# Attention beside a long convolution: one PSUM layout and one order of the turn against another

## What is computed

```
# attention: 4 heads, 2 maps each, 64 dims; latent queries see 256 + 1024 keys, context queries 256
s = einsum('bqhmd,bkhmd->bhmqk', q, k) * DIFF_SCALE
p = softmax(s, -1)
o = einsum('bhqk,bkhe->bqhe', p[:, :, 0] - lam * p[:, :, 1], v)      # then rms norm, * silu(gate)
# hyena: two long convolutions by FFT, 512 channels
z = x1 * fft_long_conv(v, kf[:, 0], bias[0]);  out = x2 * fft_long_conv(z, kf[:, 1], bias[1])
```

## Time and profile before

| | |
|---|---|
| median of 3 runs | 3829.0 us (3826.55 to 3842.98) |
| the profiled execution | 3828.31 us |
| its span, first to last instruction | 3826.5 us |
| mean granted TensorE clock | 0.953 of full speed |
| busy share of the span | TensorE 88%, VectorE 62%, ScalarE 28%, GpSimd 28% |

### The profile page before, as it was taken

One profiled execution on the slowest core, in us unless ns is written; L12 is line 12 of the kernel. 1 busy time (PEld: TensorE's weight loads), 2 busy tenths in 40 slices (PEclk: granted clock), 3 DMA queues, 4 the chain that ended last, 5 costly groups with the idle time before them and its releaser, 6 DMA issues. The chain is left out here.

```text
span 3826.5 us, 48036 instructions
## 1 busy us (share of the span) xinstructions
PE 3363.5 (88%) x18212; PEld 2736.8 (72%) x18212; DVE 2391.5 (62%) x3952; ACT 1088.9 (28%) x1980; POOL 1065.3 (28%) x766
## 2 busy tenths in 40 slices
PE   6999999999968885886997888999999588858698
PEld 2788888888758784654783576888888588845477
DVE  4134566765459986885554324557865489968765
ACT  2112222212245554332211211222221355523321
POOL 4233334333202322210122423433443022232121
PEclk8999999999979998998998899999999799989899
DMA  5354223223173222334426155323332633133441
GB/s 205 72 157 149 81 93 96 89 90 91 54 211 100 79 69 99 114 106 137 155 77 220 50 121 170 98 76 94 100 100 74 202 92 94 44 109 112 130 151 64
DMA packets 414889, 423.30 MB, mean 111 GB/s; under 512 B 57040, under 2 KB 351440, under 8 KB 413506
## 3 DMA queue, kind: packets, MB, share of 16 engines
q1 hardware_dynamic: 368676, 315.22, 28.5%
q10 hardware_dynamic: 45984, 105.01, 7.8%
HBM read 287.76 MB, written 124.01 MB: 108 GB/s over the span
## 5 line engine op out<-in xcount | busy, mean ns | idle before, releaser
L763 PE MATMUL l_p_acc<-l_u_hi,l_w_hi 128*128 128x512 f32 (+1 forms) x2208 | 605.8, 376 | 25.6 <-ACT l_p_stg L827 10.8
L763 PE MATMUL l_p_acc<-l_u_hi,l_w_lo 128*128 128x512 f32 (+1 forms) x2208 | 587.3, 367 | 0.0
L763 PE MATMUL l_p_acc<-l_u_lo,l_w_hi 128*128 128x512 f32 (+1 forms) x2208 | 586.4, 367 | 0.0
L763 PEld LDWEIGHTS l_p_acc<-l_u_hi,l_w_hi 128*128 128x128 f32 x2208 | 383.6, 189 | 102.5 <-issue 28.7
L676 POOL TENSOR_TENSOR l_w_hi<-l_wt,l_p_zero 128x1024 fp32r<-128x1024 f32 x100 | 199.6, 1996 | 916.4 <-PE l_p_acc L763 762.0
L763 PEld LDWEIGHTS l_p_acc<-l_u_hi,l_w_lo 128*128 128x128 f32 x2208 | 380.9, 189 | 71.7
L763 PEld LDWEIGHTS l_p_acc<-l_u_lo,l_w_hi 128*128 128x128 f32 x2208 | 380.5, 188 | 71.7
L1493 PE MATMUL l_at_pS<-l_at_k_hi,l_at_q 128*128 128x512 f32 (+1 forms) x400 | 165.8, 415 | 125.3 <-ACT l_at_prob L1609 69.9
L678 POOL TENSOR_TENSOR l_w_lo<-l_wt,l_w_hi 128x1024 fp32r<-128x1024 f32 x100 | 267.7, 2677 | 7.8
L1727 DVE TENSOR_REDUCE l_at_nmax<-l_at_pS 128x1 f32<-128x1280 f32 (+1 forms) x144 | 197.4, 1371 | 115.9 <-PE l_at_pS L1494 113.7
L2444 PE MATMUL l_o_pA<-l_o_w_hi,l_o_o_hi 128*128 128x512 f32 x576 | 223.6, 407 | 43.1 <-DVE l_o_o_lo L2554 31.2
(11 more groups left out here) (321 smaller groups left out, 6932.2 us busy)
## 6 DMA issues: line engine op xcount, KB each, us to landing
l_wt<-w_in SPq DMA_DIRECT2D x104, 512.0 KB, 3.9
l_n_wa<-w_ada SPq DMA_DIRECT2D x10, 2048.0 KB, 16.6
kf_d<-l_p_R SPq DMA_DIRECT2D x72, 256.0 KB, 3.7
xbc_d<-l_p_fin ACTq DMA_DIRECT2D x28, 640.0 KB, 3.0
l_at_K<-kf_d SPq DMA_DIRECT2D x64, 256.0 KB, 2.9
l_o_rows<-w_out SPq DMA_DIRECT2D x32, 512.0 KB, 4.5
l_o_oT<-o_d SPq DMA_DIRECT2D x16, 1024.0 KB, 6.8
qk_d<-l_p_late ACTq DMA_DIRECT2D x12, 1280.0 KB, 4.6
```

What stands on the lines that cost most here:

```text
L763: mm = pe.matmul(acc[:, a:a + w], (w_hi, w_lo)[wp][m % 2][:, k], (u_hi, u_lo)[up][:, k, t0 + c:t0 + c + w], start=(k == n == 0), stop=(k = ...
```

## The change

pS grows to six banks, three for each map (`MAP`), and both maps take their pieces in the same order, the 256-key piece last, with no wait on the exp of the other map. pO loses its own bank and moves into the unused half of the sixth bank, beside the last piece of map 1. So two waits are new: scores(i, 1) waits, ahead of its third piece, until norm(i-3) has read pO, and values(n) waits until exp(n+2, 1) has read that bank.

TensorE's turn becomes: values(i-3) (it was values(i-2), late in the turn); turn(i-2, 0); forward(n); turn(i-2, 1); scores(i, 1); the last batch of turn(i-2); turn_rows; scores(i+1, 0) (it was scores(i, 0), ahead of forward); backward(n). ScalarE's turn becomes: copy_back(n-1), exp(i, 0), norm(i-3), copy(i-2, 0), copy(i-2, 1), the last copy, exp(i, 1). VectorE's order stays.

```diff
@@ -1385,10 +1385,11 @@
-        pS = ps(nc, ctx, tag + "pS", 5 * BANK)
+        pS = ps(nc, ctx, tag + "pS", 6 * BANK)
+        pO = pS[:, 5 * BANK + CTX:5 * BANK + CTX + P]
         pT = ps(nc, ctx, tag + "pT", BANK)
-        pO = ps(nc, ctx, tag + "pO", BANK)
         pH = ps(nc, ctx, tag + "pH", BANK)
+        MAP = 3 * BANK
@@ -1485,11 +1486,10 @@ scores(n, m)
-                    pieces = [(0, CTX)] if q < CT else [(0, BANK), (BANK, BANK), (2 * BANK, CTX)] if m == 0 else [(CTX, BANK), (CTX + BANK, BANK), (0, CTX)]
-                    for c, w in pieces:
-                        out = pS[:, m * T + c:m * T + c + w]
-                        if w == CTX and q >= CT and n + m:
-                            pe.wait_ge(exped, 2 * n + m)
+                    for c, w in [(0, CTX)] if q < CT else [(0, BANK), (BANK, BANK), (2 * BANK, CTX)]:
+                        out = pS[:, m * MAP + c:m * MAP + c + w]
+                        if m == 1 and c == 2 * BANK and n >= 3:
+                            pe.wait_ge(scaled, n - 2)
@@ -1519,10 +1519,10 @@ values(n)
                     if n:
                         pe.wait_ge(scaled, n)
+                    pe.wait_ge(exped, 2 * min(n + 3, NU))
+                    pe.wait_ge(turned_copied, before[n + 1])
                     for kt in range(keys(q) // P):
-                        if kt % 4 == 0:
-                            pe.wait_ge(turned_copied, before[n] + kt // 4 + 1)
-                        mm = pe.matmul(pO[:, 0:P], mixT[:, kt], v_s[:, h % 2, kt], start=(kt == 0), stop=(kt == keys(q) // P - 1))
+                        mm = pe.matmul(pO, mixT[:, kt], v_s[:, h % 2, kt], start=(kt == 0), stop=(kt == keys(q) // P - 1))
@@ -1569,10 +1569,12 @@ TensorE's turns
                     turning = batches[i - 2] if 2 <= i < NU + 2 else 0
+                    if i == 0:
+                        scores(0, 0)
+                    if 3 <= i < NU + 3:
+                        values(i - 3)
                     if turning > 1:
                         turn(i - 2, 0, False)
-                    if i < NU:
-                        scores(i, 0)
                     if n is not None:
                         forward(n)
@@ -1581,7 +1583,6 @@
                     if turning:
                         turn(i - 2, turning - 1, i >= 4)
-                        values(i - 2)
@@ -1592,6 +1593,8 @@
                         turn_rows(r)
+                    if i + 1 < NU:
+                        scores(i + 1, 0)
                     if n is not None:
                         backward(n)
@@ -1644,14 +1647,14 @@ ScalarE's turns
                         copy_back(step_of(i - 1))
+                    if i < NU:
+                        exp(i, 0)
+                    if 3 <= i < NU + 3:
+                        norm(i - 3)
                     if turning > 1:
                         copy(i - 2, 0)
-                    if 3 <= i < NU + 3:
-                        norm(i - 3)
                     if turning > 2:
                         copy(i - 2, 1)
-                    if i < NU:
-                        exp(i, 0)
                     if turning:
                         copy(i - 2, turning - 1)
```

More of the change, by code:

```diff
@@ L1608, in exp @@
                         act.wait_ge(mixed, n + m - 1)
-                    act.activation(prob[:, (2 * n + m) % 3, 0:keys(q)], pS[:, m * T:m * T + keys(q)], ACT.Exp,
+                    act.activation(prob[:, (2 * n + m) % 3, 0:keys(q)], pS[:, m * MAP:m * MAP + keys(q)], ACT.Exp,
                                    bias=nmax[:, n % 2, m:m + 1], accum_out=sums[:, n % 4, m:m + 1]).then_inc(exped, 1)
@@ L1620, in norm @@
                     act.activation(small_sq[:, n % 2:n % 2 + 1], sums[:, n % 4, 0:1], ACT.Square, scale=math.sqrt(RMS_EPS)).then_inc(squared, 1)
-                    act.activation(junk[:], pO[:, 0:P], ACT.Square, accum_out=ss[:, n % 2:n % 2 + 1]).then_inc(squared, 1)
+                    act.activation(junk[:], pO, ACT.Square, accum_out=ss[:, n % 2:n % 2 + 1]).then_inc(squared, 1)
                     act.wait_ge(squared, 2 * n + 2)
@@ L1628, in norm @@
                         act.wait_ge(o_turned, n - 1)
-                    act.activation(o_t[:, n % 2], pO[:, 0:P], ACT.Copy, scale=rms[:, n % 2, 1:2]).then_inc(scaled, 1)
+                    act.activation(o_t[:, n % 2], pO, ACT.Copy, scale=rms[:, n % 2, 1:2]).then_inc(scaled, 1)
                 def copy_rows(n):
@@ L1726, in maximum @@
                     dve.wait_ge(scored, 2 * n + m + 1)
-                    dve.tensor_reduce(nmax[:, n % 2, m:m + 1], pS[:, m * T:m * T + keys(q)], AX.X, ALU.max, negate=True).then_inc(maxed, 1)
+                    dve.tensor_reduce(nmax[:, n % 2, m:m + 1], pS[:, m * MAP:m * MAP + keys(q)], AX.X, ALU.max, negate=True).then_inc(maxed, 1)
                 def combine(n):
```

## The result

The changed kernel took 3924.8 us (median of 4 runs, 3918.1 to 3928.2), against 3830.1 for the kernel before beside it: a ratio of 1.0231, 95% interval 1.0211 to 1.0250. It is slower, as forecast, but by 95 us where 50 were forecast, and so above the range's end of 3905. The profiled run took 3924.19 us, its span 3922.4, at a mean granted clock of 0.945 (0.953 before).

A forecast was written before the change was run, and what follows sets the result against it. It took VectorE and TensorE, both close to full in the attention and hyena stage, as the bound. Layer 1 +26.5, layer 0 +27.7 and first turns -3.2 made +51 on 3828.3: 3879, put down as 3878, range 3852 to 3905 us.

The forecast's parts named there:

- the chain: Inside a turn, from max(i,0) to max(i,1) through reduce, exp(i,0), norm(i-3), copy(i-2,0), transposes and a map: 6.69 us.
- D to M: Start of max(i,0) to that of max(i,1); before, 4.57, 4.73, 4.58, 6.71 us for s=(i-3) mod 4 of 3, 0, 1, 2.
- The floor: VectorE's time after the start of max(i,1), taken as before: 4.47, 6.13, 4.89, 4.78 us for s=3, 0, 1, 2.
- After the change TensorE is busy over 75% of each turn, more than in that stretch, so I keep 1.00: TensorE in the changed stage: granted clock stays 1.00, though an earlier stretch with a 2.91 us stall got 0.79.
- for s=2 nothing: Turns with (i-3) mod 4 = 2: VectorE waits nothing for max(i,1), turn stays 11.49 us.
- only s=3 grows there, by 0.35: Turns 3 to 13, row transposes waiting for the gate: only turns with s=3 grow further, by 0.35 us.
- 0 (bounds -6 to +6): Layer 0, twelve turns touching a unit of context (256 keys): no net change, bounds -6 to +6 us.
- short maps shorten the rest: Layer 0's turns touching a context unit: short maps offset a path ending at norm, about 4.9 against 4.57 to 4.73 us.
- Cost nothing: values(i-3) at the head of TensorE's turn, waiting for exp(i-1,1): no cost, with 0.3 us of cover.
- A: Rival, faster: VectorE runs at its floor and max(i,1) never waits, 3808 us; chance 0.04.
- B: Rival, no change: the chain exists without norm in it, D to M 5.28 us, time 3828 to 3832; chance 0.06.
- Case C: Rival, slower yet: TensorE's clock falls at its wait before turn(i-2,1), about 3985 us, or 3930 for half the turns; chance 0.05.

The follow-up runs named there:

- experiment 5: The changed kernel with forward's sixteen matmuls issued twice in every turn from 14 on: 3937.7 us, ratio 1.0274 to the kernel before.
- experiment 1: The changed kernel with ScalarE's old order (copy of batch 0, norm, copy of batch 1, exp of the first map): 3850.0 us, ratio 1.0041.
- experiment 10: The changed kernel with ScalarE's old order, turn_rows behind backward, and GpSimd's last level of an element waiting for VectorE's join: 3823.6 us, ratio 0.9969.

## Why the prediction was right in direction and wrong in size

The mechanism forecast, the chain, came as forecast. Its sum left out two things that came on top, the fall of the clock and the longer join, and priced several turns of layer 0 too low.

**Right.** The chain through exp(i,0), norm(i-3) and copy(i-2,0): 6.74 us measured against 6.69 summed. That nothing waits ahead of max(i+1,0) in late turns, that TensorE's idle moves to the transposes of mix, and that the values cost nothing in the late turns. They did wait, 0.62 us after turns 17, 21 and 25, where the prediction had a cover of 0.3 us, but with no effect on D to M. "The floor" after M was 0.15 too short in s=3 and s=1 (4.62 and 5.04 us).

**Wrong, in layer 1.** The forecast for the stage was 24.9 us (26.5 less 1.6 for the first turns); it grew by 45.1. By the same turns:

- Turns 16 to 30: 188.5 us measured, 175.4 by the forecast's own turns (three with s=0, four of each other). Of these 13.1 us the clock took 7.6 (the sum of D to M over 6.74 in the seven turns with s = 1 or 3 where it was longer; in all seven the transposes still start at D + 4.9; experiment 5 gives back 7.7). The failed step is "After the change TensorE is busy over 75% of each turn, more than in that stretch, so I keep 1.00". It compared a mean over a turn and passed over the one wait inside it: in turns 20, 24 and 28 TensorE was busy 75% of the turn, against 64% in the stretch of before that was granted 0.79, and the clock fell all the same, to 0.74, 0.74 and 0.87.
- In the same turns the step "for s=2 nothing" failed: D to M was 7.57, not 6.71, four times, 3.7 us with what turn 29 had besides. The mix of 2.4 us of the kernel before was no length of its own. It was a join of 1.55 us partly beside GpSimd's work, which began 0.88 us before D while VectorE idled. When the idle time went, so did the head start: GpSimd began with D, and the join took 3.28. So 0.85 of the 1.01 us that were to be won in s=2 never existed. It is the same in experiment 1.
- Joins of 6.74 for 6.69 and the tails made the last 1.8.
- Turns 3 to 15: 156.9 against 154.7 by the forecast. The three turns with s=2 took 13.19, 12.34 and 12.35 us for 11.49, and "only s=3 grows there, by 0.35" was low: turn 10 took 13.00 us for 11.51. In turn 9 TensorE had waited 2.30 us ahead of the rows, the way back behind them ran slowly (13 matmuls in 2.78 us, where 16 took 1.95 a turn later), and the products of turn 10 waited 3.40 us for forward. Turn 3 made most of it good (9.25 for 12.82).
- The drain with turn 31: 5.0 us against 2; the first turns 0.3 against -1.6.

**Wrong, in layer 0.** The stage grew by 53.2 us against 26.1 (27.7 less 1.6). The terms of the 27.1 us between them:

- The twenty whole turns grew by 23.9 us for 17.5. In turns 12, 16, 22, 24, 26 and 32 D to M was over 6.74 by 6.0 us in all, with the transposes at D + 4.9 as in layer 1 and the matmuls behind them slow: the clock again.
- The twelve turns that touch a unit of context grew by 8.6 us where I took "0 (bounds -6 to +6)". That "short maps shorten the rest" did not hold. In turn 9 the path was another one: the products waited 3.98 us for forward, which stands behind the value product, and D to M was 7.67 us for 4.72. The other eleven were not followed.
- Turns 35 and 36 took 14.09 and 13.50 us instead of 12.8 and 11.6. In turn 36 it was the clock (D to M 8.11). In turn 35 the clock held, and "Cost nothing" for the value product at the head failed: norm had to wait for it and began at D + 4.05 instead of D + 2.83, and D to M was 7.96.
- D to M of turn 37 went from 4.74 to 8.17, which stood in no term, and the two last context units took 17.6 us instead of 15 (from max(37,1) to max(39,1)).
- The first turns lost 1.0 us where 1.6 were to be won.

**The rivals.** A and B did not come. Case C had its place right, TensorE's wait at turn(i-2,1), and a chance of 0.05 that the stretch with 0.79 in the earlier trace rows did not bear out: that stretch held a single stall of 2.91 us, and the new waits are 0.9 to 3.3 us long and come once in every late turn. It came in eight of the 15 late turns, on top of the forecast chain. C's price for half the turns, some 3930, lies near the measured time by luck: it put 52 us on the forecast for the clock, and the rows give the clock about 15, namely 7.6 in the late turns of layer 1, and in layer 0 6.0 in the six turns above and 1.4 in turn 36. The rest of the miss came from terms that C did not have. The rule of the Trainium skill, "TensorE: Matmul & The Clock Gate", section "HAM oscillation — how this bites in real kernels", that waits between bursts can bring the clock down time after time, agrees with the 0.91 of turns 16 to 30 and with their 1.00 once the waits were filled.

## What to carry to other kernels

When an engine's order is changed, write the chain through every in-order queue first; the chain came out within 0.05 us of its sum where the clock held, and the forecast built on it held about half of this loss. Then, where a stretch of the old trace shows the clock fallen around a stall of the length of the new wait, price the fall, whatever the busy share of the turn. And take a duration that overlaps another engine's work on the same memory (SBUF here) not as a property of the instruction: an idle time removed ahead of it may come back inside it.

## What the hardware showed that I had not expected

- The join of 1280 columns on VectorE takes 1.55 us alone, 2.45 in the kernel before and 3.28 in turn 21 above, and its rows fit a block rather than a slowing. GpSimd's product L1680 starts at 3301.33, ahead of the join (3301.75), and ends at 3303.69; from there to the join's end at 3305.03 are 1.34 us, as in the kernel before (3231.72 to 3233.07, 1.35). GpSimd's next instruction, L1162 on 128 by 128, is issued at 3303.64 and shows 1.71 us, ending at 3305.35 behind the join, where the ones after it take 0.46. The reduce, which reads PSUM, was not held up: at 3299.85 it takes 1.49 us with GpSimd at work, as at 3286.63 without. In experiment 10 the next instruction of VectorE with all operands in SBUF met the product instead (L1774, 2.59 us for 0.67). The Trainium skill, "SBUF — State Buffer", section "Terms", under "shared port pair", says that the two engines take one pair of ports by turns, each for a whole instruction, and that "the loser **fully blocks**"; these rows agree. By that rule the join of 2.45 us in the trace of before could have been read as a join behind a product.
- More matmuls made 15 turns 7.7 us shorter, by keeping the granted clock at 1.00.
